# A two-layer hybrid trunk: bonus sums behind v's first tile, masks in four pieces on POOL, no state update behind the last chunk

## The reference

```
p = h @ w_in                                   # 512 x 3856
# RWKV-7 half
p = p + (token_shift(p) - p) * mu
r, k, v, wd, ad, gd = split_cols(p, RWKV_SIZES)
kk = l2_normalize((k * k_k).reshape(B, T, H, N))
o = rwkv7_scan(r_h, log_decay, k_h, v_h, -kk, kk * a_h)
bonus = jnp.sum((r_h * k_h * r_k), axis=-1, keepdims=True) * v_h
o = (group_norm(o) + bonus) * g
# gated DeltaNet half
qkv = jax.nn.silu(causal_depthwise_conv(qkv, conv_w))
q, k = l2_normalize(q), l2_normalize(k)
o = chunk_gated_delta_rule(q, k, v, g, beta)   # chunks of 64, a state of 64 x 64 per head
o = rms_norm(o, norm_w) * jax.nn.silu(z)
```

## Time and profile before

| | |
|---|---|
| median of 3 runs | 1552.9 us (1550.43 to 1553.49) |
| the profiled execution's own time | 1550.74 us |
| its span, first to last instruction | 1548.3 us |
| mean granted TensorE clock | 0.967 |
| busy share of the span: PE, PEld, DVE, ACT, POOL | 93%, 75%, 44%, 39%, 37% |

### The profile page before, as it was taken

One profiled execution on the slowest core, in us unless ns is written; L12 is line 12 of the kernel. 1 busy time (PEld: TensorE's weight loads), 2 busy tenths in 40 slices (PEclk: granted clock), 3 DMA queues, 4 the chain that ended last, 5 costly groups with the idle time before them and its releaser, 6 DMA issues.

```text
span 1548.3 us, 24568 instructions
## 1 busy us (share of the span) xinstructions
PE 1446.0 (93%) x10321; PEld 1158.1 (75%) x10321; DVE 682.0 (44%) x1063; ACT 605.1 (39%) x872; POOL 572.3 (37%) x265
## 2 busy tenths in 40 slices
PE   7999899888769999999999799987999999999998
PEld 5787578777758788888888687754467888888886
DVE  4665676777554312213143405877823413132231
ACT  5525463434344423223133335467844313232231
POOL 5343231101023434343434332326944443434441
PEclk9999898999869999999999899998999999999999
DMA  4332110000113232323233222210012232223231
GB/s 141 95 96 68 55 28 3 3 3 3 57 43 95 82 109 82 109 82 106 84 101 90 67 83 69 82 55 1 1 55 83 98 93 93 97 86 104 83 106 55
DMA packets 128392, 110.00 MB, mean 71 GB/s; under 512 B 10678, under 2 KB 126512, under 8 KB 128304
## 3 DMA queue, kind: packets, MB, share of 16 engines
q1 hardware_dynamic: 127712, 107.64, 22.4%
q10 hardware_dynamic: 592, 1.07, 0.2%
HBM read 106.60 MB, written 2.10 MB: 70 GB/s over the span
## 4 chain that ended last, share of the span: by engine, by line
PE 78%; DVE 11%; ACT 5%; issue 3%; POOL 2%; DMA 1%; DVEq 0%; ACTq 0%; SPq 0%; POOLq 0%
PE ps L501 21%; PE ps L506 21%; PE ps L502 21%; PE ps L637 5%; DVE lower L1874 2%; DVE lower L1870 1%; POOL lower L2083 1%; PE ps L652 1%; PE ps L645 1%; PE ps L741 1%; ACT lower L1371 1%; PE ps L614 1%; PE ps L538 1%; PE ps L948 1%; DVE lower L1653 1%
## 5 line engine op out<-in xcount | busy, mean ns | idle before, releaser
L2051 POOL TENSOR_TENSOR w_lo<-lower,w_hi 128x2048 fp32r<-128x2048 f32 x84 | 387.4, 4612 | 637.2 <-ACT w_hi L1027 637.2
L501 PE MATMUL ps<-h_hi,w_hi 128*128 128x512 f32 x792 | 315.9, 399 | 8.9 <-ACT h_hi L1032 5.9
L502 PE MATMUL ps<-h_hi,w_lo 128*128 128x512 f32 x792 | 314.5, 397 | 0.0
L1027 ACT ACTIVATE w_hi<-lower 128x2048 fp32r<-128x2048 f32 x84 | 160.2, 1907 | 242.8 <-PE ps L506 242.8
L506 PE MATMUL ps<-h_lo,w_hi 128*128 128x512 f32 x792 | 201.6, 395 | 0.4
L502 PE MATMUL ps<-a_hi,w_lo 128*128 128x512 f32 x480 | 189.1, 394 | 0.0
L501 PE MATMUL ps<-a_hi,w_hi 128*128 128x512 f32 x480 | 189.1, 394 | 0.0
L501 PEld LDWEIGHTS ps<-h_hi,w_hi 128*128 128x128 f32 x792 | 150.3, 190 | 46.5 <-issue 11.5
L502 PEld LDWEIGHTS ps<-h_hi,w_lo 128*128 128x128 f32 x792 | 150.2, 190 | 36.0 <-issue 0.5
L506 PEld LDWEIGHTS ps<-h_lo,w_hi 128*128 128x128 f32 x792 | 148.7, 188 | 37.4 <-DVE h_lo L1576 1.8
L1819 DVE TENSOR_TENSOR lower<-lower,ps 128x512 f32<-128x512 f32 x64 | 44.0, 687 | 268.7 <-PE ps L506 268.7
(11 more groups left out here) (356 smaller groups left out, 1992.4 us busy)
## 6 DMA issues: line engine op xcount, KB each, us to landing
lower<-in_mlp_w_dram SPq DMA_DIRECT2D x64, 1024.0 KB, 5.4
lower<-in_ev_w_in_dram SPq DMA_DIRECT2D x30, 512.0 KB, 3.8
lower<-in_od_w_in_dram SPq DMA_DIRECT2D x10, 1024.0 KB, 5.0
lower<-in_ev_w_out_dram SPq DMA_DIRECT2D x4, 1024.0 KB, 5.1
lower<-in_od_w_out_dram SPq DMA_DIRECT2D x4, 1024.0 KB, 5.1
out_dram<-lower SPq DMA_DIRECT2D x4, 512.0 KB, 3.2
lower<-in_od_w_in_dram SPq DMA_DIRECT2D x6, 256.0 KB, 3.8
upper<-in_x_dram SPq DMA_DIRECT2D x1, 1024.0 KB, 7.8
```

What stands on the lines that cost most here:

```text
L501: pe.matmul(o, wh, xh, start=(i_ == 0), stop=False)
L502: pe.matmul(o, wl, xh, start=False, stop=False)
L1027: act.activation(WH[:, u % 2, :, 0:w], RAW[:, u % 2, :, 0:w], ACT.Copy).then_inc(hi_ready, 1)
L2051: pool.tensor_tensor(WL[:, u % 2, :, 0:w], RAW[:, u % 2, :, 0:w], as_f32(WH[:, u % 2, :, 0:w]), ALU.subtract)\
```

## The change

Three edits. First, of the bonus sums and gq's sums TensorE now makes gq's first, then v's first tile, then the bonus sums; `plan`, the list of tiles (v's first tile is now `GV0`, the others `GV1`) and VectorE's order follow. Second, POOL makes the low parts of tiles 3, 4 and 5 between pieces of the masks and not behind them. Third, behind the last chunk of the last step the states are no longer brought up to date.

```
-                ("V", 4, 0), ("cum", 1, 1), ("GQ", 4, 0), ("kk", 4, 1), ("GK", 4, 0), ("bon", 4, 0),
-                ("gq", 4, 1), ("GV", 4, 0), ("gk", 4, 1), ("Z", 4, 0))
+                ("V", 4, 0), ("cum", 1, 1), ("GQ", 4, 0), ("kk", 4, 1), ("GK", 4, 0), ("gq", 4, 1),
+                ("GV0", 1, 0), ("bon", 4, 0), ("GV1", 3, 0), ("gk", 4, 1), ("Z", 4, 0))
...
@@ TensorE, the projection
             head_sums0("kk", SQ_KK)
             for u in range(19, 23):
                 tile(u)
+            pe.wait_ge(sq_grp, 2)
+            head_sums0("gq", SQ_GQ)
+            tile(23)
             pe.wait_ge(bonus_in, 4)
             head_sums0("bon", [BON[:, c, :] for c in range(4)])
-            pe.wait_ge(sq_grp, 2)
-            head_sums0("gq", SQ_GQ)
-            for u in range(23, 27):
+            for u in range(24, 27):
                 tile(u)
...
@@ TensorE, the recurrence
             def chunk_out(s):
+                pe.wait_ge(r_u, 2 * s + 2)
+                pe.wait_ge(r_y, 2 * s + 2)
                 both_halves(6, RK[s], VR[s % 2], True)
...
+                if behind and ahead:
+                    state_sums(m, 1)
                 if behind:
-                    state_sums(m, 1)
                     chunk_out(m)
...
-            pe.wait_ge(e_state, 2 * TT + 1)
+            pe.wait_ge(e_state, 2 * TT)
...
@@ VectorE
+            convolved("GV0", 0, 8)
             for c in range(4):
                 q = pq["bon"] + c
                 dve.tensor_tensor(BON[:, c, :], filled0(q), V[:, c, :], mul).then_inc(p_read[0], 1)
-            for c in range(4):
-                convolved("GV", c, 8 + c)
-                if c == 0:
-                    dve.wait_ge(rs_grp, 2)
-                    dve.scalar_tensor_tensor(out=wide(GQ), in0=wide(GQ), scalar=float(HD) ** -0.5,
-                                             in1=wide(Z), op0=mul, op1=mul)
+            dve.wait_ge(rs_grp, 2)
+            dve.scalar_tensor_tensor(out=wide(GQ), in0=wide(GQ), scalar=float(HD) ** -0.5,
+                                     in1=wide(Z), op0=mul, op1=mul)
+            for c in range(3):
+                convolved("GV1", c, 9 + c)
...
-                if behind:
+                if behind and ahead:
                     solved(m, 1)
...
-                if behind:
+                if behind and ahead:
                     state_sums(m, 1)
...
@@ POOL
+            tile_lo(3)
             first = FULL[:, 0, :].rearrange("p (n q) -> p n q", q=2)[:, :, 1]
             t.link(pool.memset(first, -1.0))
             select(first, 0, [[-2, P // 2]], 1, 0.0, ALU.is_equal)
             for lev in range(1, LEVELS):
+                if lev == 3:
+                    tile_lo(4)
...
+            tile_lo(5)
             for g in range(16):
...
-            for u in range(3, len(tiles)):
+            for u in range(6, len(tiles)):
                 tile_lo(u)
```

More of the change, by code:

```diff
@@ L320, in trunk_kernel @@
         tiles += [("K1", c, 640 + c * P, P) for c in range(3)]
-        tiles += [(n_, c, o_ + c * P, P) for n_, o_ in (("R", 0), ("V", 1024), ("GQ", GDN_QKV), ("GK", GDN_QKV + 512),
-                                                       ("GV", GDN_QKV + 1024), ("Z", GDN_Z)) for c in range(4)]
+        tiles += [(n_, c, o_ + c * P, P) for n_, o_ in (("R", 0), ("V", 1024), ("GQ", GDN_QKV), ("GK", GDN_QKV + 512))
+              for c in range(4)]
+        tiles += [("GV0", 0, GDN_QKV + 1024, P)] + [("GV1", c, GDN_QKV + 1152 + c * P, P) for c in range(3)]
+        tiles += [("Z", c, GDN_Z + c * P, P) for c in range(4)]
         tile_q = [pq[n_] + c for n_, c, _, _ in tiles]
@@ L1056, in silu0 @@
             def silu0(i):
-                act.wait_ge(p_read[0], p_reads(pq[("GQ", "GK", "GV")[i // 4]] + i % 4))
+                act.wait_ge(p_read[0], p_reads(tile_q[15 + i]))
                 act.activation(GQKV[:, i, :], GQKV[:, i, :], ACT.Silu).then_inc(conv_used, 1)
```

## The result

The changed kernel takes 1543.8 us by the median of 5 runs (1542.63 to 1544.56); the kernel before, run beside it, 1552.67 us (5 runs, 1547.45 to 1553.49). The ratio is 0.995, 95% interval 0.9933 to 0.9967. In a second series it was 0.9956 (0.9941 to 0.9971), with 1543.95 against 1550.91. So the kernel became faster by 7 to 9 us, where 3.5 had been forecast and 1546.0 was the low end of the range.

What follows compares the result with a forecast made beforehand. TensorE, busy 93% of the span, was taken as the bound, with gains only where it waits or runs slow: 2.2 + 0.7 + 0.6 = 3.5 us, 1547.2 on the profiled execution, 1549.4 on the median's footing; range 1546.0 to 1552.3.

Steps and rivals of the forecast that it cites:

- The footing: Whole kernel: the median of the runs before lies 2.2 us above the profiled execution, so 1547.2 became 1549.4.
- POOL's masks: Start: with masks in pieces, tile 3's low part comes sooner and TensorE begins at 32.7, 2.2 us gained.
- Bonus sums behind v's first tile: Projection: v's first tile fills TensorE's wait; tile 24 ends at 186.0 against 186.74, 0.7 us gained.
- No last state update: Last chunk: work is removed, but L1692 is held by POOL's instruction and ends at about 438.6, 0.6 us gained.
- the 0.7 us of L1698: Last chunk: this instruction (L1692 before) taking 0.7 us, not stretched to some 3, would show the forecast wrong.
- an unheld L1692: Last chunk: not held by POOL, this instruction makes the part worth some 3 us; shares a 0.17 chance, 1547.0.
- the second part gives nothing: Projection: fourth bonus sum waits longer on ScalarE or the clock stays low through tile 24; 1551, chance 0.22.
- POOL comes late: Start: low part late for tile 4 or 6, a 1 to 2 us wait taking back most of 2.2; 1551, chance 0.05.
- the kernel becomes slower: Projection: gq's first read, at 184.2, makes the kernel 3.5 us slower, 1556.4; chance 0.06.
- The first rival: Tile 24 or last chunk: the clock is not lost, or L1692 is not held; 1547.0, chance 0.17.
- its second branch: Last chunk: L1692 not held, 2.2 + 0.7 + 3 = 5.9 us gained; within a shared chance of 0.17.
- the clock elsewhere: Recurrence and both projections: the prediction fails if TensorE's low stretches change by more than 3 us in sum.

Runs made afterwards that it cites:

- c_only: Only the last state update left out, against the kernel before: 1550.21 us, ratio 0.9986.
- a_only: Only POOL's masks cut into pieces, against the kernel before: 1548.75 us, ratio 0.9985.
- b_again: Repeat series of only the new order of head sums, v's first tile and VectorE, against the kernel before: 1548.6 us, ratio 0.9988.
- gap_before: Kernel before, update kept, with ScalarE's first output-weight high part and POOL's low part brought forward: 1551.56 us, ratio 0.9998 to before.
- pool_first: Changed kernel with ScalarE's weight high part early and POOL held until just ahead of the output's products: 1544.31 us, ratio 0.9957 to before.
- pool_gap: Changed kernel with ScalarE's weight high part early and POOL's low part ending before L1698 starts: 1538.99 us, ratio 0.9935 to before.

## Why the prediction was off

The sign was right, and so were the mechanisms at the start and at v's first tile. That of the last chunk holds in `c_only` and not in the changed kernel. The size was half of what was measured. Of the 5.6 us between 1549.4 and 1543.8, 1.5 are the footing and 2.4 the last chunk; the remaining 1.7 are not placed by any profile, and the second part's surplus is the likely place:

- **The footing, 1.5 us.** The forecast stood on a median of three runs, 1552.9. Series of 29 and 32 runs have 1551.3 and 1551.5. The forecast from the profiled execution, 1547.2, was the better one.
- **POOL's masks: right.** Reckoned 2.2; 2.1 at tile 3 in the first profile (0.7 to 0.9 in the second), 2.3 by the ratio of `a_only`. All three low parts came in time, as did tile 6's at 45.79.
- **Bonus sums behind v's first tile: right where it was reckoned, mis-sized for the kernel.** The fourth sum was put at 177.3 in the clock of the profile before, which is 174.5 here less 2.2 and 0.57; it came at 174.75. Tile 24 took 7.7 us where 7.6 was taken. It ends 186.74 - 183.57 = 3.2 earlier, of which 2.1 is the masks' (2.0 by the end of tile 22), 0.57 the start, and 0.5 to 0.6 this part's; 0.7 was the term. (In the profile of `b_again`, 212.0 us to the last read of Z beside 212.3 and 211.9 of before, next to nothing of it is left.) (The 2.1 us that tile 24 was to lose were taken over from tile 23 as they stood; the 3.2 us at the low clock that stand beside them explain 1.6 of it.) But the kernel is 1.9 and 3.7 us faster by its two series. The step that failed is in the sum: it adds three terms to the profiled execution and puts the code behind the projection at nothing, as if it cost the same at all times. It doesn't: in the profiles of the second part 2.0 to 3.8 us were gained in the recurrence and behind it. Part of that is the run and not the edit, as `c_only` shows. Why the rest goes with this part is open; what the record shows is a granted clock that is high in more of the runs.
- **No last state update: mis-sized.** The step that failed is "L1692 ... now starts inside the same POOL instruction, which nothing moves", and with it "at most 96/48 of 2.82, 5.6 us: 434.7 (at the pace of before, 4.3)". The output's products took 2.8 us, because the clock came back at 425.1, and L1698 was 0.23 us ahead of POOL; the 0.7 us of L1698 had been named as a sign of being wrong. `c_only`, where POOL was first, shows the 0.6 that was reckoned; the changed kernel shows 15.37 - 12.37 = 3.0. Of the 2.4 between them 1.4 is TensorE's clock and 1.1 the order at the port. The 3.0 that stood among the rivals for an unheld L1692 was met in part by luck: VectorE was held all the same, four instructions later, for 2.15 us.
- **The rivals.** That the second part gives nothing, that POOL comes late and that the kernel becomes slower all fell: the first read of gq's sums came 4.8 us behind the SiLU, not 8. The first rival was nearest: 5.9 by its second branch, and by the ratios 6.8 to 7.8 was measured.

The forecast named the clock elsewhere as what would make it fail, "by more than 3 us in sum", and gave the range only one microsecond for it. Two profiles of before and one of `gap_before` lie within 0.7 us behind the last read of Z; `b_again`, which changes nothing there, lies 3.8 below, and `c_only` 3.9 below before in the recurrence alone. A bound for it would have been some 4 us, on the side of gain at least.

The Trainium skill (SBUF — State Buffer, "Who interferes with whom") says that issue order decides which of the two blocks. The traces agree: L1698, 0.23 us ahead, was not held and POOL's instruction took 4.83 for 4.50, while L1698 behind it took 3.43 in `pool_first`. The same section lets `tensor_reduce` go free and counts `tensor_scalar` among those that can take the shared pair; here L1702, a reduce, took 0.67 inside POOL's instruction and L1703, a tensor_scalar, 2.32.

## What to carry to other kernels

When an instruction is removed from a place where two costs lie beside each other, reckon each pair: here the update and the port collision were worth 0.6 and 0.3 us alone and 3.9 together. Where VectorE and POOL meet at their shared port within a microsecond, reckon the stretch for either clock of TensorE (1.4 us apart here) and for either order (0.6 to 1.1); better, move POOL's instruction into a time when VectorE waits for TensorE: `pool_gap` took another 2.2 us out of this stretch, and the kernel went from 1543.95 to 1538.99, though the intervals of the two ratios overlap. Give the range of a kernel whose granted clock is 0.97 the few microseconds by which the clock's low stretches can move behind any reordering and from run to run. Base the forecast on many runs of before or on its profiled execution, and don't read a gain of 1 to 2 us in an untouched stretch from a single pair of profiles.

## What the runs showed of the hardware that was not expected

- TensorE's clock in one and the same code differs from run to run, and an edit elsewhere shifts how often it is high: 19 of 84 runs of before have a mean of 0.969 or more, 19 of 22 with the second part. Within the kernel before the two groups are 3.5 us apart.
- An instruction of 128x8 can be the one that is held: L1703, 2.32 us for 0.17, while L1702 (a reduce) took 0.67 inside the same instruction of POOL, and L1699 and L1701, with one input in PSUM, 0.69 each.
- A meeting at the port costs VectorE's part of the tail 2.2 us when VectorE comes first (9.57 against 7.41) and 2.75 to 3.3 when POOL does (10.16 to 10.70).
